# Sample attention loads its first values at its begin and weighs one key chunk sooner; the merge runs in pieces of 512, 512 and 64

## What is computed

```python
def fox_sample(q, k, v, logf, cache_k, cache_v, cache_logf, page_table):
    kp = cache_k[page_table].reshape(DB, past, H, Dh)      # 8 x 2048 x 8 x 64
    vp = cache_v[page_table].reshape(DB, past, H, Dh)
    ...
    s_past = jnp.einsum('bqhd,bkhd->bhqk', q, kp) * scale
    s_past = s_past + suffix[:, :, None, :] + cn[:, :, :, None]
    s_new = jnp.einsum('bqhd,bkhd->bhqk', q, k) * scale
    s_new = s_new + cn[:, :, :, None] - cn[:, :, None, :]
    s_new = jnp.where(causal, s_new, -jnp.inf)
    p = jax.nn.softmax(jnp.concatenate([s_past, s_new], axis=-1), axis=-1)
    return (jnp.einsum('bhqk,bkhd->bqhd', p[..., :past], vp)
            + jnp.einsum('bhqk,bkhd->bqhd', p[..., past:], v))

def merge_branches(x, a_out, b_out, ga, gb, w_up_a, w_up_b, w_o):
    m = ga * (a_out @ w_up_a) + gb * (b_out @ w_up_b)
    return x + m @ w_o
```

## Time and profile before

| what | us |
|---|---|
| median of 3 runs | 1987.73 |
| lowest and highest | 1986.86, 1989.68 |
| the profiled execution | 1991.32 |
| its span, first to last instruction | 1989.7 |
| sample attention, first instruction to merge's first | 746.6 to 951.4 |
| merge, first instruction to the next stage's first | 951.4 to 1078.5 |

### The profile page before, as it was taken

The page is one execution under the profiler, slowest core; times in us unless marked ns, Lnnn a source line. Parts: engine busy times, 40 slices in busy tenths (PEclk is TensorE's granted clock), DMA queues, the critical chain, the costliest instruction groups (busy, mean ns, idle before and its releaser), DMA issues. The chain is left out here.

```text
span 1989.7 us, 22766 instructions
## 1 busy us (share of the span) xinstructions
PE 1892.0 (95%) x8401; PEld 989.0 (50%) x8401; DVE 602.4 (30%) x1414; ACT 296.3 (15%) x514; POOL 190.1 (10%) x275
## 2 busy tenths in 40 slices
PE   8999999899999998998999997999999999996997
PEld 4454445556566655665555444544444444442443
DVE  4201114333334334553232223411111111110777
ACT  2000001122222222333110111400000000000000
POOL 1000004200000002443000000100000000000331
PEclk9999999899999997999999998999999999998999
DMA  7102110351121227999421242689999999997242
GB/s 269 15 18 71 46 43 1 141 192 65 49 69 44 69 70 255 370 381 379 175 68 54 75 184 107 254 341 430 418 419 418 426 420 419 420 426 269 85 143 79
DMA packets 109456, 406.77 MB, mean 204 GB/s; under 512 B 19017, under 2 KB 36490, under 8 KB 97058
## 3 DMA queue, kind: packets, MB, share of 16 engines
q1 hardware_dynamic: 84546, 327.33, 42.5%
q0 software_dynamic: 16496, 56.15, 7.7%
q10 hardware_dynamic: 8304, 21.84, 2.8%
HBM read 354.48 MB, written 50.79 MB: 204 GB/s over the span
## 5 line engine op out<-in xcount | busy, mean ns | idle before, releaser
L2078 PE MATMUL psum<-arena 128*64 128x512 f32 (+1 forms) x1024 | 341.1, 596 | 1.4 <-DVE arena L2172 1.4
L835 PE MATMUL psum<-arena 128*128 128x363 f32 (+1 forms) x768 | 254.9, 477 | 5.0 <-ACT arena L866 5.0
L2078 PEld LDWEIGHTS psum<-arena 128*64 128x64 f32 (+1 forms) x1024 | 129.3, 164 | 178.9 <-issue 177.0
L294 PE MATMUL psum<-arena 128*128 128x512 f32 x432 | 188.7, 596 | 0.0
L835 PEld LDWEIGHTS psum<-arena 128*128 128x128 f32 x768 | 140.4, 192 | 78.9 <-ACT arena L866 7.7
L2117 PE MATMUL psum<-arena 128*64 128x512 f32 (+1 forms) x512 | 170.0, 596 | 1.0 <-DVE arena L2186 1.0
L294 PEld LDWEIGHTS psum<-arena 128*128 128x128 f32 x432 | 82.0, 192 | 99.3 <-issue 99.3
L1553 PE MATMUL psum<-arena 128*128 128x512 f32 x288 | 127.2, 597 | 1.6 <-PEq L1385 1.6
L2423 PE MATMUL psum<-arena 128*128 128x512 f32 x288 | 127.2, 601 | 1.4 <-DVE arena L2455 1.4
L2117 PEld LDWEIGHTS psum<-arena 128*64 128x64 f32 (+1 forms) x512 | 66.2, 164 | 101.8 <-issue 101.8
L2172 DVE TENSOR_TENSOR arena<-psum,g_moe_rows 128x1024 f32<-128x1024 f32 x24 | 29.4, 1224 | 250.4 <-PE psum L2072 250.4
(11 more groups left out here) (278 smaller groups left out, 1856.9 us busy)
## 6 DMA issues: line engine op xcount, KB each, us to landing
arena<-in_w_exp_gate SPq DMA_DIRECT2D x32, 2048.0 KB, 13.6
arena<-in_w_exp_up SPq DMA_DIRECT2D x32, 2048.0 KB, 14.2
arena<-in_w_exp_down SPq DMA_DIRECT2D x32, 2048.0 KB, 10.8
arena<-in_cache_k SPq DMA_DIRECT2D x128, 256.0 KB, 6.7
arena<-in_cache_v POOLq DMA_DIRECT2D x128, 256.0 KB, 7.6
moe_out<-arena ACTq DMA_DIRECT2D x24, 512.0 KB, 11.8
arena<-in_w_in SPq DMA_DIRECT2D x5, 2048.0 KB, 19.9
moe_out<-arena SPq DMA_DIRECT2D x1, 10240.0 KB, 34.9
```

The lines of the kernel that those rows point to most:

```text
L294: last = mm(c.bank[4 + r % 3][:, :], HT[:, k, t * P:(t + 1) * P], W[:, n + 1, k, :], start=(k == 0), stop=(k == KD - 1))
L835: done = mm(c.bank[7][:, 0:b - a], WG[blk % 2][:, k, q * P:(q + 1) * P], HT[:, k, a:b], start=(k == 0), stop=(k == KD - 1))
L2078: last = mm(out[rows_, :], XT[:, u % 2, k, rows_], c.ring_tile(LOAD[kind, u, r])[:, k, :], start=(k == 0), stop=(k == KD - 1))
```

## The change

Five things are edited.

1. Page numbers of sample 0's values are read by POOL in the prompt's attention stage. In sample attention POOL sets `QB` and `CN` to zero, issues the 16 DMAs of sample 0's values, and then sets `AT8` to zero. DVE still waits for all three.
2. `CN` and sample 0's `SUF` are loaded by ACT at the head of its list, not by SP. SP loads sample 1's `SUF` behind sample 1's keys.
3. `w_up_a` and `w_up_b` are loaded behind that, ahead of sample 2's keys.
4. The second half of sample b - 1 moves one key chunk forward on TensorE, ACT and DVE.
5. Merge cuts the tokens in pieces of 4 tiles, 4 tiles, and the 64 rows of the samples.

```diff
@@ -773,6 +773,8 @@
         def _(pool):
             pool.wait_ge(c.out_rows, 16 * 7)
             nc.gpsimd.memset(zeros, 0.0).then_inc(blank, 1)
+            pool.wait_ge(c.pages_in, 16)
+            c.v_numbers = [c.page_numbers(pool, 0, ch) for ch in range(NCH)]
 
         @block.tensor
         def _(pe):
@@ -1032,43 +1034,45 @@
     def strip(j):
         return slice(j * STRIP, (j + 1) * STRIP)
 
+    def load_suffix(eng, b):
+        for ch in range(NCH):
+            keys = slice(ch * 512, ch * 512 + 512)
+            eng.dma_start(SUF[bias_rows(ch), b % 2, keys], c.sufd[:, b, keys]).then_inc(bias_in[b % 2], 16)
+
     with nc.Block() as block:
         @block.sync
         def _(sp):
-            sp.wait_ge(zeroed, 3)
-            for h in range(H):
-                at = STRIP * (h // 2) + DT * (h % 2)
-                sp.dma_start(CN[at:at + DT, :], c.cum_d[h:h + 1, SEQ:].to_broadcast([DT, NS])).then_inc(cn_in, 16)
             sp.wait_ge(c.sufd_out, 16 * H)
-            for b in range(DB):
+            for b in range(1, DB):
                 if b >= 2:
                     sp.wait_ge(chunk_mm, NCH * (b - 1))
-                for ch in range(NCH):
-                    keys = slice(ch * 512, ch * 512 + 512)
-                    sp.dma_start(SUF[bias_rows(ch), b % 2, keys], c.sufd[:, b, keys]).then_inc(bias_in[b % 2], 16)
-                if b == 0:
-                    continue
+                    load_suffix(sp, b)
                 for ch in range(NCH):
                     sp.wait_ge(k_tr, U * (b - 1) + NPAIR * (ch + 1))
                     c.load_keys(sp, b, ch)
-            for n, w in enumerate((c.w_up_a, c.w_up_b)):
-                sp.dma_start(view(c, UP_AT + n * WBLK, KF, D), w).then_inc(c.up_in, 16)
+                if b == 1:
+                    load_suffix(sp, 1)
+                    for n, w in enumerate((c.w_up_a, c.w_up_b)):
+                        sp.dma_start(view(c, UP_AT + n * WBLK, KF, D), w).then_inc(c.up_in, 16)
 
         @block.gpsimd
         def _(pool):
             g_ = nc.gpsimd
+
+            def load_values(numbers, ch):
+                for g in range(CH):
+                    pool.dma_start(VC[:, ch, g, :], c.cache_v[bass.ds(numbers[ch][g] * P, P), :]).then_inc(v_in[ch], 16)
+
             g_.memset(QB, 0.0).then_inc(zeroed, 1)
+            g_.memset(CN, 0.0).then_inc(zeroed, 1)
+            for ch in range(NCH):
+                load_values(c.v_numbers, ch)
             g_.memset(AT8, 0.0).then_inc(zeroed, 1)
-            g_.memset(CN, 0.0).then_inc(zeroed, 1)
-            pool.wait_ge(c.pages_in, 16)
-            for b in range(DB):
+            for b in range(1, DB):
                 numbers = [c.page_numbers(pool, b, ch) for ch in range(NCH)]
                 for ch in range(NCH):
-                    if b >= 1:
-                        pool.wait_ge(v_used, NCH * (b - 1) + ch + 1)
-                    for g in range(CH):
-                        pool.dma_start(VC[:, ch, g, :], c.cache_v[bass.ds(numbers[ch][g] * P, P), :]
-                                       ).then_inc(v_in[ch], 16)
+                    pool.wait_ge(v_used, NCH * (b - 1) + ch + 1)
+                    load_values(numbers, ch)
 
         @block.tensor
         def _(pe):
@@ -1178,16 +1182,16 @@
                 next_keys(NCH * b + 1)
                 if b >= 2:
                     turn_out(b - 2)
-                next_keys(NCH * b + 2)
                 if b >= 1:
                     turn_weights(b - 1, 0)
                     turn_weights(b - 1, 1)
-                next_keys(NCH * b + 3)
+                next_keys(NCH * b + 2)
                 if b >= 1:
                     turn_weights(b - 1, 2)
                     turn_weights(b - 1, 3)
                     turn_own(b - 1)
                     weigh(b - 1)
+                next_keys(NCH * b + 3)
             scores(NCH * DB - 1)
             turn_out(DB - 2)
             for q in range(4):
@@ -1223,17 +1227,23 @@
                 s.activation(SN[:, p, :], SN[:, p, :], ACT.Exp, bias=low[:, p:p + 1], scale=-1.0,
                              accum_out=sums[:, p, 1:2]).then_inc(exps, 1)
 
+            act.wait_ge(c.sufd_out, 16 * H)
+            load_suffix(act, 0)
+            act.wait_ge(zeroed, 2)
+            for h in range(H):
+                at = STRIP * (h // 2) + DT * (h % 2)
+                act.dma_start(CN[at:at + DT, :], c.cum_d[h:h + 1, SEQ:].to_broadcast([DT, NS])).then_inc(cn_in, 16)
             for b in range(DB):
                 keep_keys(b, 0)
+                if b >= 1:
+                    exp(b - 1)
                 keep_keys(b, 1)
                 if b >= 1:
-                    exp(b - 1)
+                    keep_weights(b - 1, 0)
                 keep_keys(b, 2)
                 if b >= 1:
-                    keep_weights(b - 1, 0)
+                    keep_weights(b - 1, 2)
                 keep_keys(b, 3)
-                if b >= 1:
-                    keep_weights(b - 1, 2)
             exp(DB - 1)
             keep_weights(DB - 1, 0)
             keep_weights(DB - 1, 2)
@@ -1349,15 +1359,15 @@
                 bias(NCH * b)
                 if b >= 2:
                     out_cells(b - 2)
+                if b >= 1:
+                    keep_weights(b - 1, 1)
                 keep_keys(b, 2)
                 bias(NCH * b + 1)
                 if b >= 1:
-                    keep_weights(b - 1, 1)
+                    keep_weights(b - 1, 3)
+                    keep_own(b - 1)
                 keep_keys(b, 3)
                 bias(NCH * b + 2)
-                if b >= 1:
-                    keep_weights(b - 1, 3)
-                    keep_own(b - 1)
             bias(NCH * DB - 1)
             lowest(DB - 1)
             out_rows(DB - 2)
@@ -1380,7 +1390,7 @@
     sig, a_mm, b_mm = c.sem("gates_sig"), c.sem("up_a_mm"), c.sem("up_b_mm")
     prod_a, prod_b, m_done, m_pad = c.sem("prod_a"), c.sem("prod_b"), c.sem("m_done"), c.sem("m_pad")
     c.wo_in = c.kept_sem("wo_in")
-    cuts = ((0, 3), (3, 6), (6, NT))
+    cuts = ((0, 4), (4, NP), (NP, NT))
     NPC = 3 * KD
     with nc.Block() as block:
         @block.sync
@@ -1401,16 +1411,17 @@
             pe.wait_ge(c.up_in, 32)
             for p in range(NPC):
                 col, (a, b) = p // 3, cuts[p % 3]
+                n = P if b <= NP else NS
                 if p >= 4:
                     pe.wait_ge(prod_a, p - 3)
                 for k in range(KF):
-                    last = mm(c.bank[p % 4][:, 0:(b - a) * P], UPA[:, k, col * P:(col + 1) * P], AT[:, a:b, k, :],
+                    last = mm(c.bank[p % 4][:, 0:(b - a) * n], UPA[:, k, col * P:(col + 1) * P], AT[:, a:b, k, 0:n],
                               start=(k == 0), stop=(k == KF - 1))
                 last.then_inc(a_mm, 1)
                 if p >= 4:
                     pe.wait_ge(prod_b, p - 3)
                 for k in range(KF):
-                    last = mm(c.bank[4 + p % 4][:, 0:(b - a) * P], UPB[:, k, col * P:(col + 1) * P], BT[:, a:b, k, :],
+                    last = mm(c.bank[4 + p % 4][:, 0:(b - a) * n], UPB[:, k, col * P:(col + 1) * P], BT[:, a:b, k, 0:n],
                               start=(k == 0), stop=(k == KF - 1))
                 last.then_inc(b_mm, 1)
```

## The result

The changed kernel takes 1997.53 us (median of 6 runs, 1990.96 to 2003.97) against 1988.7 us before on the same chip (1986.86 to 1992.63). The ratio is 1.0046 (95% interval 1.0025 to 1.0067), so it is slower by 5 to 13 us, where 1988.7 was forecast and 1993.0 was the upper end of the range. The sign of the sum (+1.0) was right, its size was not, and "same" had the largest chance.

The account below looks back on a forecast made before the run. TensorE's order bounds sample attention, transfers just behind; TensorE bounds merge. 8.1 - 0 - 0.3 - 1.2 - 4.8 - 0.3 - 0 - 0.5 = +1.0 us on 1987.7 gives 1988.7, range 1982.5 to 1993.

Parts of the forecast that it names:

- the sum: Whole kernel: all terms together make it +1.0 us, 1988.7 us for the median.
- "same": Whole kernel: a time that can't be told from no change, within 0.2% (4.0 us); chance 0.68.
- Step 1: First samples: DVE's first key copy 9.2 us late, a new bias wait of 3.8, sample 1 goes on 8.1 late.
- Step 2: Middle samples: 21.88 us each instead of 22.19; -0.3 for sample 1 and -1.2 for samples 2 to 6.
- since 401 was reached, I take -1.2: Samples 2 to 6: transfers can follow at 386 GB/s, so -1.2 us, between ends 0 and -1.55.
- The lower end, 0: Samples 2 to 6: the end of the estimate at which the shorter samples gain nothing, 0 us.
- Step 3: `w_up` ahead of sample 2's keys: they still land in time, cost 0, cover 6 us.
- Step 4: Stage's end: waits for values go; -4.8 us, and -0.3 for sample 7's own order.
- The wait of 2.78 us goes: no `w_up` beside the values: Stage's end: the wait for values at 931.96 disappears; part of the -4.8 us.
- Step 5: Merge: TensorE 0 with 64-column matmuls 0.108 us apart; DVE's shorter tail gives -0.5 us.
- Rival D: Sample 2's keys: `w_up` before them on SP's queue, TensorE waits 9 us, 1997.7 us; chance 0.10.

Follow-up runs that it names:

- at8_first: The changed kernel with `AT8` set to zero ahead of the 16 value loads; ratio to before 1.0017.
- order_half_values: The kernel before with only the new order (weighted sum ahead of the fourth chunk's transposes), loading half of each value row in samples 2 to 6; ratio 0.9974.
- bias_ahead: The changed kernel with sample 1's bias rows loaded by SP ahead of sample 1's keys, as before the change; ratio to before 1.0060.
- both_starts: The changed kernel with `AT8` set to zero ahead of the value loads and sample 1's bias rows ahead of its keys; ratio to before 1.0026.
- ups_alone: The kernel before with only the two `w_up` loads moved from the stage's end to behind sample 1's keys; ratio 1.0030.
- merge_alone: The kernel before with only merge's pieces changed, to 512, 512 and 64 columns; ratio 1.0009.
- after: The changed kernel, all five edits against the kernel before, in its first runs and profile; 1997.53 us, ratio 1.0046.
- ups_last: The changed kernel with `w_up` loaded at the stage's end again, all else as in the change; ratio to before 1.0045.
- again: The changed kernel measured and profiled once more, nothing altered; ratio to before 1.0037.

## Why the prediction was wrong

**Step 1, the start: right in mechanism, 1.8 us too dear.** DVE's first copy was forecast 9.2 us late, at 757.6; less the 5.0 us by which this execution is ahead, that is 752.6, and it came at 752.70. The wait for the bias, not for keys, and the half-speed stretch came as forecast. The wait was 5.6 us instead of 3.8: TensorE was there at 772.4 and not at 775.6, since its clock had risen earlier in sample 0, while SP's chain and the landing gave the rows at 778.0, where 779.4 was forecast. at8_first shows DVE's hold to be the larger part of the loss.

**Step 2, the middle: the failed step, with step 4.** The order does give 21.85 us for a sample where it runs free (21.88 forecast; at least one sample in each run with that order). What failed is "since 401 was reached, I take -1.2". The window at 401 GB/s holds `w_up`'s two loads of 2 MB; in the windows of 22 us with keys and values alone I read 372 to 381. At 379 a sample needs 22.3 us, about what the kernel before already took (22.19). The term was mis-sized: +0.7 was measured for -1.2, with three of the five samples at 22.6 to 22.7 us and waits for keys of 0.76, 0.69 and 0.57 us in them. The lower end, 0, was the right one; order_half_values shows that fewer bytes free the samples, and how much SP's chain adds is open. The 0.7 us are of the size of chance: nine rows of the table lie between 110.6 and 111.7.

**Step 3, `w_up` at sample 2: right for this kernel, for another reason.** No wait came, and the margin was 5.0 us (6 forecast), but it was the bias wait's gift. bias_ahead, both_starts and ups_alone showed waits for sample 2's keys (9.4, 11.5 and 4.0 us in sum) as soon as TensorE was there in time. I should have summed the bytes up to sample 2's keys without the delays that the same change brings.

**Step 4, the end: the failed step.** -5.1 was forecast and -1.6 measured. "The wait of 2.78 us goes: no `w_up` beside the values" was true, and worth nothing. I took the wait as time on the path. In the profile of before and in ups_alone the path at the end is `weigh` of sample 6, 1.8 us to the first issue, 17 to 18 us until the last page has landed, and the last chunk of sample 7: ups_alone has no wait inside sample 6 and all of them in sample 7, and from the start of `weigh` of sample 6 to merge's first matmul it takes 25.9 us, where the kernel before takes 951.47 - 926.35 = 25.1. It is not so in every execution: merge_alone, with the same code there, waits 3.68 us inside sample 6 and not at all in sample 7, and is at half speed for the 13.7 us from 923.7 on. But the end is 40.5 us without `w_up` beside the values and 39.7 or 41.1 with it. I had priced POOL's issues at 9.45 us, from the burst at the begin; they take 11.8, as POOL reads page numbers between the first and the second.

In after the values are not what ends the stage: the last page landed at 943.9, and no wait for it is left. With `w_up` back at the end (ups_last) it is the same, 38.0 us against 38.1, so there too the move of `w_up` gave nothing. The forecast had 13.8 us from X7 to `weigh` of sample 6, 16.4 to that of sample 7, and 10.0 - 2.1 = 7.9 to merge; after took 15.4, 17.6 and 8.7. The first is the wait of 1.58 us for keys. The other two are TensorE's own work: the fourth chunk now stands behind `weigh`, with a wait of 0.78 us for ACT's copy of its last keys that I had left out, and the clock was at half speed from 937.9 to 944.7, over the turned weights (3.87 us) and the begin of `weigh` (4.59 us, against 3.70 at the full clock). What is left, -1.6, is about the 1.4 us by which the end differs between before and merge_alone, which have the same code there. What the order does by itself shows in the 15.4 us, against 18.2 in both of those.

**Step 5, merge: right.** 64-column matmuls start (1076.48 - 1075.65)/8 = 0.104 us apart, 0.108 forecast from the MLP's row. The Trainium skill's 25 ns (TensorE: Matmul & The Clock Gate, "Back-to-back issue gap") are for a matmul by itself; the same section says that at small sizes this figure under-counts where each matmul has its own weight load, and the trace agrees: 0.104 us, not 0.025. The tail gained 0.1 us and not 0.5: DVE's last operation now begins at 1077.91 and takes 0.23 us, but TensorE starts the next stage at 1078.60, against 1078.69.

**The sum.** By profiles +6.0 + 0.7 - 1.6 - 0.1 = +4.9 us (the parts are rounded). Against the forecast of +1.0 that is 1.8 less at the start, 1.9 more in the middle, 3.5 more at the end and 0.4 more in merge. On the 1987.7 us of the prediction it gives 1992.6, still inside the range; by medians the change is +8.8 and +8.4 us, and that is outside. The 4 us between them are not located. A part may be the one profile of before: merge_alone has the same sample attention and takes 203.5 us for it, against which the change's stage is 6.4 and 7.2 us longer. Samples whose clock fell are not the answer in the profile that we have: again is 6.5 us longer than after, but 0.8 of it in this stage, 1.4 in merge and 4.3 in the stages behind it. Rival D had the time almost to the digit (1997.7), and that is luck: in after no sample waits for `w_up`.
